# Shorter and fewer unread fp32 products in the long product stretches of TensorE

## Chip, cores and metric

The kernel runs on one core of one Trainium2 chip. Its time is device microseconds of that core, and a comparison is made between medians of several executions.

## The reference

Two networks are applied one after the other to x, 512 tokens of width 1024. Cut to what matters here:

```
def first_block(x, ...):
    for l in range(2):
        m = even_mixer(x, ...) if l % 2 == 0 else odd_mixer(x, ...)
        x = layer_norm(ALPHA * x + m, ...)
        x = layer_norm(ALPHA * x + conv_ffn(x, ...), ...)

def second_block(x, mem, ...):
    x = x + hybrid_mixer(rms_norm(x), ...)               # SSD scan, windowed attention, two gated branches
    x = x + memory_cross_attention(rms_norm(x), rms_norm(mem), w_q, w_kv, w_o)
    x = x + swiglu_ffn(rms_norm(x), w_in, w_out)
    return rms_norm(x, norm_final_g)
```

Nearly all of the arithmetic is in the products with large fp32 weight matrices: the two mixers' projections in and out, two convolutional feed-forward blocks (1024 to 5632 and 2816 back to 1024), the memory's keys and values, the hybrid mixer's input, its branches and its output, the cross attention's projections, and a last feed-forward block.

## The kernel before

**Units and tiles.** All weight matrices come as one stream of 405 units of 128 x 1024 fp32 (8 blocks of 128 x 128), 512 KB each, through a ring of four slots. SyncE issues the loads, ScalarE rounds a unit to `w_hi` (L323), VectorE forms the remainder `w_lo` (L329), and TensorE uses both. An output tile has 128 output channels and 512 tokens. For each block of 128 input channels `product_tile` issues three terms, `w_hi` with x high, `w_hi` with x low, `w_lo` with x high, each as two products of 256 columns (L357): six products a block, 48 a unit. In the profile they stand as groups of four with `w_hi` and two with `w_lo`.

**Stages.** TensorE walks the stages in a fixed order that is written out by hand (`pe_stages`): even_in, retention and stick-breaking attention, even_out, up0, down0, odd_in, differential attention, odd_out, up1, down1, norms with the memory's keys and values (xkv), bcdt, ssd, br_ssd, qkv, windowed attention, br_attn, mix_out, cross attention, xout, ffn_in, ffn_out. Products of layer-norm tails and heads are issued by `half_tile` (L388), those of two attention stages in parts (L1362), those of the memory from L1710.

**Plain fp32 products.** Small work (transposes, sums over partitions by a matrix of ones, attention scores) runs as plain fp32 products. In the profile one such product stands as two records, so a pair of them is four.

**The unread products.** `settle(pe, bank)` (L334 to L337) issues two fp32 products, ones by 256 columns of ones, into a bank of `ps` that nobody reads then. `product_tile` calls it when its argument `spare` names a bank, at the places of `SETTLE` (L332): ahead of block 0, term 0, and ahead of block 4, term 1. `spare` is given once in each of six stages, in an early tile: even_in (bank 3, tile (1, 1)), up0, odd_in and up1 (`head_pe`, bank 4, tile (1, 1)), br_ssd (bank 3, j == 1) and br_attn (bank 0, j == 1). That is 6 stages x 2 places x 2 products = 24 products. In down1, after tile 4, `mem_sum_pe` sums the memory over partitions (one fp32 product of 256 columns, L1653), and one unread product of 256 columns follows it (L1129). The stage xout has none; `xout_pe` issues its tiles 2 to 7.

Of the kernel before, what the change touches and what calls it, by code (L numbers as in the profile page):

```python
# [26 lines left out]
P = 128  # L27
# [31 lines left out]
UB, TB = {}, {}  # L59
# [22 lines left out]
CONST = {}  # L82
# [12 lines left out]
HALF = 256  # L95
# [93 lines left out]
def ffn_stage_numbers(stage):  # L189

    return {"up0": 0, "down0": 0, "up1": 1, "down1": 1, "ffn_in": 2, "ffn_out": 2}[stage]


def build(nc, dram, out):
    ctx = ExitStack()
    with ctx:
# [12 lines left out]
        const = ctx.enter_context(nc.sbuf_tensor("const", [P, N_CONST], F32))  # L209
        small = ctx.enter_context(nc.sbuf_tensor("small", [P, 128], F32))  # L210
        acc = [ctx.enter_context(nc.psum_tensor(f"acc{b}", [P, S], F32)) for b in range(2)]
        ps = ctx.enter_context(nc.psum_tensor("ps", [P, 6, S], F32))
        ident = const[:, CONST["ident"]:CONST["ident"] + P]
        ones = const[:, CONST["ones"]:CONST["ones"] + P]
# [68 lines left out]
        def ev(name):  # L283
            name = SHARED.get(name, (name, 0))[0]
            if name not in s:
                s[name] = sem(name)
            return s[name]
# [41 lines left out]
            dve.tensor_tensor(w_lo[:, u.slot], w_raw[:, u.slot], w_hi[:, u.slot].bitcast(F32),  # L329
                              ALU.subtract).then_inc(lo_done, 1)  # L330

        SETTLE = ((0, 0), (4, 1))  # L332

        def settle(pe, bank):  # L334

            for _ in range(2):
                pe.matmul(ps[:, bank, 0:HALF], ones, const[:, CONST["ones"]:CONST["ones"] + HALF], start=True, stop=True)  # L337

        def product_tile(pe, u, t, hi, lo, blocks=(8,), n=S, ready=None, spare=None):


            pe.wait_ge(acc_free[t.bank], t.in_bank + 1)
            a, k, total = acc[t.bank], 0, sum(blocks)
            parts = [slice(at, at + HALF) for at in range(0, n, HALF)]
            for m in blocks:
                pe.wait_ge(lo_done, u.count + 1)
                for b in range(m):
                    if ready is not None:
                        pe.wait_ge(ev(ready[0]), ready[1] + k + 1)
                    wh = w_hi[:, u.slot, b * P:(b + 1) * P]  # L350
                    wl = w_lo[:, u.slot, b * P:(b + 1) * P]
                    for term, (w, x) in enumerate(((wh, hi), (wh, lo), (wl, hi))):
                        if spare is not None and (k, term) in SETTLE:
                            settle(pe, spare)
                        for h in parts:

                            mm = pe.matmul(a[:, h], w, AR[:, x + k, h], start=(k == 0 and w is wh and x == hi and h.start == 0),  # L357
                                           stop=(k == total - 1 and w is wl), skip_group_check=True)
                    k += 1
                mm.then_inc(units_used, 1)  # L360
                u = u + 1
# [10 lines left out]
        def half_tile(pe, u, t, hi, lo, blocks, h, start=True, free=True, done=False, tail=False,  # L372
                      ready=None, between=()):


            if free:
                pe.wait_ge(acc_free[t.bank], t.in_bank + 1)
            a, k, total = acc[t.bank], 0, sum(blocks)
            cols = slice(HALF * h, HALF * h + HALF)
            for n, m in enumerate(blocks):  # L380
                pe.wait_ge(lo_done, u.count + 1)
                for b in range(m):
                    if ready is not None:
                        pe.wait_ge(ev(ready[0]), ready[1] + k + 1)
                    wh = w_hi[:, u.slot, b * P:(b + 1) * P]
                    wl = w_lo[:, u.slot, b * P:(b + 1) * P]
                    for w, x in ((wh, hi), (wh, lo), (wl, hi)):
                        mm = pe.matmul(a[:, cols], w, AR[:, x + k, cols], start=(start and k == 0 and w is wh and x == hi),  # L388
                                       stop=(k == total - 1 and w is wl), skip_group_check=True)
                    k += 1  # L390
                if done:
                    mm.then_inc(units_used, 1)
                elif tail and n == len(blocks) - 1:
                    mm.then_inc(ev("tail_a"), 1)
                if n < len(between):
                    between[n](pe)
                u = u + 1
# [7 lines left out]
        def tail_pe(pe, stage, hi, lo, blocks, c):  # L405
            r, per = TAIL[stage], len(blocks)
            norm = [lambda e: ln_sum_pe(e, c, 0, stage), lambda e: ln_var_pe(e, c, 0)]
            for h in range(2):
                for n in range(KD - r, KD):
                    between = norm[n - (KD - r):][:1] if per == 1 else norm  # L410
                    half_tile(pe, Units(UB[stage] + per * n), tail_tile(stage, n, h), hi, lo, blocks, h,
                              done=(h == 1), tail=True, between=between if h == 1 else ())
# [707 lines left out]
        def down_pe(pe, stage):  # L1120
            f = ffn_stage_numbers(stage)
            for j in range(KD - TAIL.get(stage, stage == "ffn_out")):
                product_tile(pe, Units(UB[stage] + 3 * j), Tiles(TB[stage] + j), GH, GL, DOWN,
                             ready=None if j else ("g_lo", KF * f))
                if stage == "down1" and j == 2:
                    mem_pe(pe)
                if stage == "down1" and j == 4:
                    mem_sum_pe(pe)
                    pe.matmul(ps[:, 1, 0:HALF], ones, const[:, CONST["ones"]:CONST["ones"] + HALF], start=True, stop=True)  # L1129
            if stage in TAIL:  # L1130
                tail_pe(pe, stage, GH, GL, DOWN, 1)
            if stage == "ffn_out":

                u = Units(UB[stage] + 3 * (KD - 1))
                half_tile(pe, u, Tiles(TB[stage] + KD - 1), GH, GL, DOWN, 0, tail=True)
                half_tile(pe, u, Tiles(TB[stage] + KD), GH, GL, DOWN, 1, done=True,
                          between=(lambda e: final_sum_pe(e, 0),))
                final_sum_pe(pe, 1)
# [4 lines left out]
        def final_sum_pe(pe, h):  # L1143
            pe.wait_ge(ev("sq_sum"), (KD - 1) * 4)
            pe.matmul(ps[:, 2 + h, 0:HALF], ones, A[:, SQ_SUM, last_half(h)], start=True, stop=False)
            pe.wait_ge(ev("rms_sq"), nth("rms_sq", KD * 4 + h))
            pe.matmul(ps[:, 2 + h, 0:HALF], ones, A[:, TMP + 4 + (KD - 1) % 2, last_half(h)], start=False,
                      stop=True).then_inc(ev("rms_sum"), 1)
# [494 lines left out]
        def mem_pe(pe):  # L1643
            pe.wait_ge(ev("mem_in"), 16)
            for k in range(KD):
                for c in range(MC):
                    mm = pe.transpose(mem_ps(k)[:, P * c:P * c + P],
                                      A[:, MEM_RAW + 2 * c + k // 4, (k % 4) * P:(k % 4 + 1) * P], ident)
                mm.then_inc(ev("mem_t"), 1)

        def mem_sum_pe(pe):
            pe.wait_ge(ev("mem_add"), nth("mem_add", KD))
            pe.matmul(ps[:, 2, 0:MEM], ones, A[:, MEM_SUM, 0:MEM], start=True, stop=True).then_inc(ev("mem_var"), 1)  # L1653
# [932 lines left out]
        XQ, XK, XV, XOH, XOL, X_SOFT, X_TURN = 16, 40, 48, 24, 32, TMP, 56  # L2586
# [199 lines left out]

        def xout_pe(pe):
            for n in range(2, KD):
                product_tile(pe, Units(UB["xout"] + n), Tiles(TB["xout"] + n), XOH, XOL)


        def ffn_pe(pe):
# [24 lines left out]
        def ffn_dve(dve):  # L2817
# [22 lines left out]
            input_pe, even_in_pe, ret_sb_pe,  # L2840
            lambda e: mixer_out_pe(e, "even_out", 8),
            lambda e: up_pe(e, "up0"), lambda e: down_pe(e, "down0"),
            odd_in_pe, diff_pe,
            lambda e: mixer_out_pe(e, "odd_out", 16),
            lambda e: up_pe(e, "up1"), lambda e: down_pe(e, "down1"),
            norms_pe, bcdt_pe, ssd_pe, br_ssd_pe,
            qkv_pe, win_pe, br_attn_pe, mix_pe, xattn_pe, xout_pe,
            ffn_pe, lambda e: down_pe(e, "ffn_out"),
        ]
        act_stages = [  # L2850
# [284 lines left out]
```

## Time and profile before

| | |
|---|---|
| median of 3 runs | 2666.0 us (2664.82 to 2670.92) |
| the profiled execution, its time | 2669.54 us |
| its span, first to last instruction | 2667.7 us |
| TensorE busy | 2593.1 us, 97% |
| VectorE, ScalarE busy | 1481.7 us, 1241.3 us |
| mean granted TensorE clock | 0.991 of full |
| bytes read from memory | 267 MB, 104 GB/s |
| unread products, L337 and L1129 | 48 and 2 records, 12.3 and 0.6 us of modelled busy time |

Busy time of TensorE overlaps from one product to the next, so the duration of one product (277 ns for 256 columns) is no price. The distance between the starts of successive products is: a group's time in the chain of work that ended last, divided by its count, or the distance between two starts in the timeline.

### The profile page before, as it was taken

How to read it: one execution, taken by the hardware profiler on the slowest of the kernel's cores; microseconds unless marked ns; L12 is line 12 of the kernel's file. 1: busy time of each engine (PE TensorE's matmuls, PEld its weight loads, DVE VectorE, ACT ScalarE, POOL GpSimd, SP SyncE). 2: the span in 40 equal slices, each digit the busy share in tenths (PEclk: the TensorE clock that was granted, in tenths of full speed). 3: DMA queues.
4: the chain of work that ended last, by engine and by line, in shares of the span. 5: the costliest groups of instructions: out<-in, count | busy, mean ns of one | idle time of the engine just before them, and what ended most of it. 6: DMA issues, size and time to landing. Idle time of an engine off the chain costs nothing.

```text
span 2667.7 us, 51033 instructions
## 1 busy us (share of the span) xinstructions
PE 2593.1 (97%) x20954; PEld 2395.1 (90%) x20954; DVE 1481.7 (56%) x2490; ACT 1241.3 (47%) x2037; POOL 118.0 (4%) x185
## 2 busy tenths in 40 slices
PE   8999999999999999999999999989999999999998
PEld 8985999999996699999989776779966998999998
DVE  5234666653426776664467989852476445544433
ACT  4336344432426644442365887842475243444422
POOL 0000000000000000000001233300000000000000
PEclk9999999999999999999999999999999999999999
DMA  7950233333331023333354566633311331333332
GB/s 195 116 84 1 64 104 96 98 105 107 111 96 48 25 74 102 95 97 118 105 195 142 183 197 193 198 109 96 93 50 56 96 127 48 96 96 100 95 103 72
DMA packets 75784, 279.02 MB, mean 105 GB/s; under 512 B 9402, under 2 KB 11610, under 8 KB 75088
## 3 DMA queue, kind: packets, MB, share of 16 engines
q1 hardware_dynamic: 62112, 217.42, 25.6%
q0 software_dynamic: 13488, 58.88, 10.0%
q8 instruction: 147, 2.41, 0.4%
q14 instruction: 37, 0.30, 0.0%
HBM read 267.03 MB, written 9.24 MB: 104 GB/s over the span
## 4 chain that ended last, share of the span: by engine, by line
PE 80%; DVE 11%; ACT 5%; issue 2%; DMA 1%; POOL 0%; DVEq 0%; ACTq 0%; SPq 0%
PE acc L357 66%; PE acc L388 3%; DVE big L1862 2%; DVE res_tmp L2161 1%; PE ps L388 1%; PE acc L1710 1%; DVE big L2492 1%; PE acc L1362 1%; DVE res_tmp L2155 1%; DVE w_lo L329 1%; PE ps L473 1%; DVE big L1514 1%; PE ps L779 1%; ACT res_tmp L2131 1%; ACT w_hi L323 1%
## 5 line engine op out<-in xcount | busy, mean ns | idle before, releaser
L357 PE MATMUL acc<-x_split,w_hi 128*128 128x256 f32 x7936 | 1234.0, 277 | 5.2 <-DVE big L1862 3.3
L357 PEld LDWEIGHTS acc<-x_split,w_hi 128*128 128x128 f32 x7936 | 1053.0, 188 | 8.2 <-issue 7.2
L357 PE MATMUL acc<-x_split,w_lo 128*128 128x256 f32 x3968 | 774.1, 276 | 0.0
L329 DVE TENSOR_TENSOR w_lo<-w_raw,w_hi 128x1024 fp32r<-128x1024 f32 x405 | 494.2, 1221 | 474.7 <-ACT w_hi L323 474.6
L323 ACT ACTIVATE w_hi<-w_raw 128x1024 fp32r<-128x1024 f32 x405 | 427.0, 1055 | 557.9 <-PE acc L357 519.9
L357 PEld LDWEIGHTS acc<-x_split,w_lo 128*128 128x128 f32 x3968 | 598.9, 188 | 0.0
L357 PE MATMUL acc<-big_r,w_hi 128*128 128x256 f32 x3376 | 523.4, 277 | 0.8 <-DVE big_r L2545 0.8
L357 PEld LDWEIGHTS acc<-big_r,w_hi 128*128 128x128 f32 x3376 | 447.7, 188 | 1.7 <-DVE big_r L2545 0.9
L357 PE MATMUL acc<-big_r,w_lo 128*128 128x256 f32 x1688 | 330.0, 277 | 0.0
L357 PEld LDWEIGHTS acc<-big_r,w_lo 128*128 128x128 f32 x1688 | 254.9, 188 | 0.0
L1076 ACT ACTIVATE res_tmp<-acc,par 128x512 f32<-128x512 f32 x84 | 64.9, 773 | 137.3 <-PE acc L357 132.9
L1101 DVE SCALAR_TENSOR_TENSOR res_tmp<-acc,par,res_tmp 128x511 f32<-128x511 f32 x84 | 62.8, 748 | 89.1 <-ACT res_tmp L1076 88.9
L2131 ACT ACTIVATE res_tmp<-res_tmp 128x256 f32<-128x256 f32 (+3 forms) x192 | 91.1, 550 | 34.2 <-DVE res_tmp L2155 34.0
L2161 DVE TENSOR_TENSOR res_tmp<-res_tmp 128x640 f32<-128x640 f32 x96 | 81.5, 885 | 14.0 <-ACT res_tmp L2131 13.6
L1862 DVE SCALAR_TENSOR_TENSOR big<-acc,par,big 128x510 f32<-128x510 f32 (+1 forms) x96 | 71.8, 748 | 11.5 <-ACT big L1852 8.8
L388 PE MATMUL acc<-big_r,w_hi 128*128 128x256 f32 x432 | 77.0, 282 | 0.5 <-DVE res_tmp L553 0.5
L1081 ACT ACTIVATE res_tmp<-res_tmp 128x512 f32<-128x512 f32 x44 | 27.8, 633 | 89.5 <-DVE small L1109 89.5
L1104 DVE SCALAR_TENSOR_TENSOR res_tmp<-acc,par,res_tmp 128x510 f32<-128x510 f32 x84 | 62.8, 748 | 11.7 <-DVE res_tmp L1101 0.3
L388 PEld LDWEIGHTS acc<-big_r,w_hi 128*128 128x128 f32 x432 | 66.3, 189 | 1.3 <-DVE res_tmp L553 0.9
L388 PE MATMUL acc<-big_r,w_lo 128*128 128x256 f32 x216 | 60.1, 278 | 0.0
L1978 POOL DMA_DIRECT2D res_tmp<-scratch_rows x96 | 51.3, 540 | 176.1 <-PE ps L2019 151.4
L1114 DVE TENSOR_TENSOR big_r<-res_tmp,big_r 128x512 f32 (+1 forms) x44 | 30.5, 693 | 43.8 <-ACT big_r L1083 43.8
(360 smaller groups left out, 2761.4 us busy)
## 6 DMA issues: line engine op xcount, KB each, us to landing
w_raw<-in_stream SPq DMA_DIRECT2D x405, 512.0 KB, 3.6
res_tmp<-scratch_rows POOLq DMA_DIRECT2D x96, 320.0 KB, 5.3
big<-scratch_rows POOLq DMA_DIRECT2D x32, 320.0 KB, 5.7
scratch_bias<-res_tmp POOLq DMA_DIRECT2D x8, 320.0 KB, 13.6
res_tmp<-in_x SPq DMA_DIRECT2D x2, 1024.0 KB, 6.9
res_tmp<-scratch_bias POOLq DMA_DIRECT2D x8, 256.0 KB, 4.0
scratch_x<-res_tmp POOLq DMA_DIRECT2D x1, 2048.0 KB, 8.9
scratch_kv<-big POOLq DMA_DIRECT2D x1, 2048.0 KB, 10.3
```

Of the source, the lines that this page charges most:

```text
L323: act.activation(w_hi[:, u.slot], w_raw[:, u.slot], ACT.Copy).then_inc(hi_done, 1)
L329: dve.tensor_tensor(w_lo[:, u.slot], w_raw[:, u.slot], w_hi[:, u.slot].bitcast(F32), ALU.subtract).then_inc(lo_done, 1)
L357: mm = pe.matmul(a[:, h], w, AR[:, x + k, h], start=(k == 0 and w is wh and x == hi and h.start == 0), stop=(k == total - 1 and w is wl), ...
L388: mm = pe.matmul(a[:, cols], w, AR[:, x + k, cols], start=(start and k == 0 and w is wh and x == hi), stop=(k == total - 1 and w is wl), s ...
L1076: act.activation(x, acc[t.bank][:], ACT.Identity, bias=col(f"cb{f}", tile), scale=col(f"cw{f}", tile + 88)).then_inc(ev("conv_now"), 1)
L1101: dve.scalar_tensor_tensor(x[:, 1:S], a[:, 0:S - 1], col(f"cw{f}", tile + 44), x[:, 1:S], ALU.mult, ALU.add).then_inc(ev("conv_tap1"), 1)
L1104: dve.scalar_tensor_tensor(x[:, 2:S], a[:, 0:S - 2], col(f"cw{f}", tile), x[:, 2:S], ALU.mult, ALU.add).then_inc(acc_free[t.bank], 1)
L1114: dve.tensor_tensor(AR.at(GL, 2 * i + q), prod, AR.at(GH, 2 * i + q).bitcast(F32), ALU.subtract).then_inc(ev("g_lo"), 1)
L1862: ins = dve.scalar_tensor_tensor(o, i, col("cw2", m + 24 * j), o, ALU.mult, ALU.add)
L1978: pool.dma_start(part(f, b, c), src).then_inc(ev(row_in(f, c)), 16)
L2131: ins = act.activation(w, w, ACT.Exp, bias=tab[:, 0, c, head:head + 1])
L2161: dve.tensor_tensor(w, w, cb, ALU.mult).then_inc(ev("s_w"), 1)
```

## The change

`SETTLE` keeps its first place alone, so each `spare` tile has one pair of unread products in place of two pairs. Each unread product has 128 columns in place of 256. In down1 a whole `settle` (two products of 128 columns) stands behind the memory's sum, where one product of 256 columns stood. Tile 2 of xout gets a pair (bank 0). No wait, no transfer and no other instruction is changed.

```diff
-        SETTLE = ((0, 0), (4, 1))
+        SETTLE = ((0, 0),)
 
         def settle(pe, bank):
 
             for _ in range(2):
-                pe.matmul(ps[:, bank, 0:HALF], ones, const[:, CONST["ones"]:CONST["ones"] + HALF], start=True, stop=True)
+                pe.matmul(ps[:, bank, 0:P], ones, const[:, CONST["ones"]:CONST["ones"] + P], start=True, stop=True)
...
                 if stage == "down1" and j == 4:
                     mem_sum_pe(pe)
-                    pe.matmul(ps[:, 1, 0:HALF], ones, const[:, CONST["ones"]:CONST["ones"] + HALF], start=True, stop=True)
+                    settle(pe, 1)
...
         def xout_pe(pe):
             for n in range(2, KD):
-                product_tile(pe, Units(UB["xout"] + n), Tiles(TB["xout"] + n), XOH, XOL)
+                product_tile(pe, Units(UB["xout"] + n), Tiles(TB["xout"] + n), XOH, XOL, spare=0 if n == 2 else None)
```

## Rows read from the trace of the kernel before

**Rows 1.** The page: engines, granted clock in 40 slices, shares of the chain.

```profile
PE 2593.1 (97%) x20954; PEld 2395.1 (90%) x20954; DVE 1481.7 (56%) x2490; ACT 1241.3 (47%) x2037; POOL 118.0 (4%) x185
...
PEclk9999999999999999999999999999999999999999
...
PE 80%; DVE 11%; ACT 5%; issue 2%; DMA 1%; POOL 0%; DVEq 0%; ACTq 0%; SPq 0%
```

**Rows 2.** Chain in order of time, long stretches: start us, us, what, count.

```profile
48.39 122.19 PE acc L357 x1078
...
350.91 313.95 PE acc L357 x2770
664.86 10.20 PE acc L388 x90
...
724.94 100.44 PE acc L357 x886
...
996.75 254.12 PE acc L357 x2242
...
1781.89 176.60 PE acc L357 x1558
...
2055.12 73.24 PE acc L357 x646
```

**Rows 3.** Timeline of TensorE, even_in: start us, modelled us, line, tiles, count.

```profile
42.18 0.62 PE L357 MATMUL acc<-x_split,w_hi 128*128 128x256 f32 x4
...
42.86 0.62 PE L357 MATMUL acc<-x_split,w_hi 128*128 128x256 f32 x4
...
43.54 1.02 PE L337 MATMUL ps<-const 128*128 128x256 f32 x4
...
45.10 0.62 PE L357 MATMUL acc<-x_split,w_hi 128*128 128x256 f32 x4
...
45.78 0.62 PE L357 MATMUL acc<-x_split,w_hi 128*128 128x256 f32 x4
...
46.46 0.62 PE L357 MATMUL acc<-x_split,w_hi 128*128 128x256 f32 x4
...
47.37 1.02 PE L337 MATMUL ps<-const 128*128 128x256 f32 x4
...
48.70 0.62 PE L357 MATMUL acc<-x_split,w_hi 128*128 128x256 f32 x4
```

**Rows 4.** Timeline of TensorE in ssd, round an fp32 pair of 128 columns.

```profile
1552.51 0.66 PE L2054 MATMUL ps<-const,big 128*128 128x128 f32 x4
...
1553.70 0.62 PE L357 MATMUL acc<-x_split,w_hi 128*128 128x256 f32 x4
...
1554.38 0.62 PE L357 MATMUL acc<-x_split,w_hi 128*128 128x256 f32 x4
```

**Rows 5.** Chain in order of time: behind eight and more fp32 records.

```profile
1250.86 1.75 PE ps L1647 x16
1252.61 31.09 PE acc L357 x264
...
1765.88 11.31 PE acc L357 x96
...
2255.64 3.43 PE ps L2653 x8
...
2263.31 39.58 PE acc L357 x336
```

**Rows 6.** Chain in order of time: behind four fp32 records.

```profile
301.26 2.74 PE acc L388 x24
...
317.80 2.83 PE acc L388 x24
...
1284.57 44.90 PE acc L357 x396
...
2304.61 338.66 PE acc L357 x2988
```

## The prediction

> **What bounds the kernel.** I read the page first. TensorE is busy 97% of the span and has 80% of the chain of work that ended last, and the clock digit is 9 in all forty slices, the full level of 2.4 GHz but for short stretches [rows 1]. So an instruction taken from TensorE in a dense stretch is time taken from the kernel, unless something else becomes late. Then I went through the chain in order of time, because there a group's time over its count is the true distance between starts. The reader is to see in it that the same product of 256 columns runs at two paces. In the long stretches 122.19 / 1078, 313.95 / 2770, 254.12 / 2242 and 176.60 / 1558 all give 113.3 to 113.4 ns [rows 2]. Elsewhere 31.09 / 264, 39.58 / 336 and 11.31 / 96 give 117.8 ns [rows 5]. The clock is full in both, no wait stands inside these groups, and a stretch keeps the pace with which it starts until TensorE is interrupted. The difference is 4.45 ns a product, 0.21 us a unit of 48.
>
> What chooses the pace is the thing to predict. Each of the six stages with unread products runs at the short pace behind them [rows 2], also br_ssd, which stood at 117.8 ns just ahead of them (1765.88 [rows 5]). Behind long runs of plain fp32 products the long pace is usual: 16 records of L1647, 8 of L2653 [rows 5]; of the 17 places where a run of eight or more equal records with full weights leads directly into products, 14 go on at the long pace. Behind four records the short pace is usual: x396 behind the pair in down1, which stood at 117.8 ns ahead of it [rows 5, 6], and x2988 at 113.3 ns [rows 6]. It isn't certain: of six pairs in the layer-norm heads four give 2.74 or 2.73 us for 24 products and two give 2.83, which is 117.9 ns each [rows 6]; both of these two come where TensorE had idled between products a moment before. A pair inside an unbroken stream has given the short pace at each of its 20 places, twelve of them the pairs of L337.
>
> **The second pair.** Between the first and second pairs of even_in the groups of six start at 45.10, 45.78 and 46.46: 0.68 us for six, 113.3 ns, so already the short pace [rows 3]. The other five stages show the same 0.68 there. In this trace the second pair gives nothing. Its price: without it the six-groups from 46.46 would follow at 0.68, so 48.70 would be 47.82. That is 0.88 us, and the first pair costs 45.10 - 42.86 - 1.36 = 0.88 us as well [rows 3]. Six second pairs are 6 x 0.88 = 5.3 us, all on TensorE, with nothing beside it that would hide them.
>
> **Half the columns.** The price of 0.88 us is four records and a restart of the stream. Plain fp32 records go by their columns: eight of 512 (L2653) take 3.43 us, 429 ns each, so 215 for 256 columns, and 16 of 128 (L1647) take 1.75 us, 109 ns each [rows 5]. Four records at 109 instead of 215 ns save 0.42 us, which leaves 0.46 us a pair. As the other bound, the nearest whole case is a pair of 128 columns in ssd: L2054 starts at 1552.51 and the six-group at 1553.70, where one six of 0.68 lies between, so 0.51 us [rows 4]; 0.05 of that belongs to the wider product ahead of it, so I take 0.46. Six first pairs save 6 x 0.42 = 2.5 us (2.2 with the upper bound).
>
> Does a pair of 128 columns choose the short pace too? The only cases are those in ssd. Sixteen such pairs stand directly ahead of products, and 15 of them go on at 0.68 us for six, as here from 1553.70 to 1554.38 [rows 4]; the one that does not (0.71 us) comes directly behind eight records of 512 columns, so it belongs with the long runs. Against it: there the stream had been broken by other fp32 work, while the new pairs stand inside a stream. Number of records, and not their time, is what separates the cases: the four records of 512 columns ahead of the x2988 (L1560 and L1562) take as long as eight of 256 would, and give the short pace [rows 6]. I take the short pace for all six stages.
>
> The Trainium skill ("TensorE: Matmul & The Clock Gate", Back-to-back issue gap) gives one spacing for a width, columns over 2.4 plus 2.5 ns, 109.2 ns for 256. The trace has 113.3 and 117.8 ns in its place, two values, so the rule misses what the change is about. By it pace would never be at stake, xout's pair would be a pure cost of 0.46 us, and the sum would be 5.3 + 2.5 - 0.5 = 7.3 us, 2658.7 us.
>
> **down1.** One unread product of 256 columns goes (two records, 430 ns) and two of 128 come (four records, 436 ns), with one restart as before. I take nothing; the bounds are a gain of 0.1 us, if a restart behind narrow records is shorter, and a loss of 0.1, if it is longer as in ssd. But with the memory's sum there are now six records in a row, between the four that give the short pace and the eight that give the long. If it falls to the long pace, 396 products [rows 6] cost 1.8 us. I keep this for the range.
>
> **xout.** The stretch from 2263.31 is seven tiles (336 products) at 117.8 ns [rows 5]; the pair comes ahead of the second of them, so 288 products go to 113.35 ns, a gain of 1.28 us, for 0.46 us. Net gain 0.8 us; a loss of 0.5 if the pair doesn't act.
>
> **What could hide or follow.** No wait is added, and no instruction stands behind a new one but the products themselves. The unread product writes a bank on TensorE alone. The suppliers keep up: a unit of 48 products takes 5.44 us, VectorE and ScalarE are busy 56% and 47% [rows 1], and the ring is four units deep, so 0.9 us once in a stretch finds no one late. The stages behind the stretches start from TensorE's last tile, so they move up with it.
>
> **Sum.** 5.3 + 2.5 + 0 + 0.8 = 8.6 us off. The profiled execution took 2669.54 us (span 2667.7 us), so it would be 2660.9 us. The median of the runs shown, 2666.0 us, is 3.5 us under the profiled one, and the forecast for the median is 2666.0 - 8.6 = 2657.4 us, 0.33% less. Places that restart behind an idle TensorE may choose their pace anew with shifted times; those with over 200 products are worth 1 to 2 us each, of both signs, so I put 3 us round the sum. For this kernel a change under 0.2% (5.3 us) can hardly be told from none.
>
> **Rivals.**
> The first is that the short pair leaves the pace as it finds it. For it: its four records take 0.44 us where the wide ones took 0.86, and the cases in ssd came behind broken streams. Then even_in, up0, odd_in and up1 stay short, as they were ahead of the first pair (42.18 to 42.86 is 0.68 us [rows 3]), but br_ssd (about 1584 products with the 26 between the pairs) and br_attn (672) stay long [rows 2, 5], and xout and down1 with them: (1584 + 672 + 288 + 396) x 4.45 ns = 13.1 us, and the time is 2670.5 us, the same within 0.2%. Beside it stands a rule of the Trainium skill (same page, What happens when you issue a matmul): the queue pulls weight loads ahead of products in flight, so an interruption would act by the time that it gives the queue; no row shows that queue.
>
> The second ends on the other side: the short pair puts the stream on the long pace, as the 16 records of 128 columns of L1647 did [rows 5]. The six stretches hold 1078 + 2770 + 90 + 886 + 2242 + 1558 + 646 = 9270 products [rows 2]. At 4.45 ns they cost 41.3 us, with xout and down1 44.3, and the time is 2701.7 us, 1.3% slower. It decides as soon as the loss passes 14 us, which up0 (12.7 us) does together with any other. Against it speak the 15 pairs in ssd.
>
> The third is that one stretch misses: the dropped second pair was its second throw. up0 alone gives 2670.1, up1 (10.0 us) 2667.4, br_ssd (7.0) 2664.4, even_in (4.8) 2662.2, odd_in (3.9) 2661.3, br_attn (3.0) 2660.4 us: mostly the same within 0.2%. Two of six head pairs missed [rows 6], but none of those within a stream.
>
> **Chances.** Forecast 0.70, pace left as found 0.08, long pace 0.07, one stretch missed 0.13, others 0.02. Faster by over 0.2% needs 2660.7 us or less: 0.64 of the 0.70 and 0.02 of the missed stretch, 0.66. Slower takes the 0.07, two missed stretches and the rest, 0.11. Same 0.23. The likeliest case alone spans 2654 to 2661 us. The range of 8 in 10 goes from 2653 to 2671 us: it takes in the first and third rivals and leaves out the second.
>
> **What the profile after would show.** L337 with 32 records of 128 columns, 109 ns apart (four in each of the six stages, in xout and in down1), none of 256 and no L1129. In the timeline about 0.46 us at each place. In the chain 113.3 ns a product behind each pair, in br_ssd and xout with 117.8 ahead of it. The prediction is wrong if a stretch of [rows 2] gives 117.8 ns, by 4.45 ns times its count, and its size is wrong if the restart behind narrow records is longer than in ssd.

## The result and the profile after

The changed kernel takes 2686.65 us in the median of 12 runs (2671.74 to 2698.26), the kernel before 2667.01 us (2664.16 to 2670.92, 12 runs). The ratio is 1.0066 with an interval of 1.005 to 1.0082: slower by two thirds of a per cent, where 0.33% faster was forecast, and outside the range of 2653 to 2671 us. (The two medians divide to 1.0074; the ratios in this text are those recorded with the runs.) The single times spread over 27 us, those of before over 7 us. That spread is itself a finding, and is taken up below. Three executions of the kernels below took thousands of us (one with two narrow pairs, two with one wide pair and xout); the medians of those kernels are taken without them.

The page of the changed kernel, in the lines that answer to [rows 1]:

```profile
PE 2612.1 (97%) x20936; PEld 2418.0 (90%) x20936; DVE 1482.6 (55%) x2490; ACT 1241.0 (46%) x2037; POOL 118.3 (4%) x185
...
PEclk9999999999999999999999999999999999999999
```

The clock digit is 9 throughout (mean 0.993 of full), the other engines do the same work, and TensorE is busy 19 us longer although it has fewer columns to pass. The chain of work in order of time says where (start us, us, what, count), and answers to [rows 2] and [rows 5]:

```profile
44.19 130.03 PE acc L357 x1104
...
344.36 5.66 PE acc L357 x48
350.46 316.90 PE acc L357 x2796
717.22 5.44 PE acc L357 x48
723.10 107.43 PE acc L357 x912
...
989.54 5.44 PE acc L357 x48
995.43 267.13 PE acc L357 x2268
...
1296.27 44.90 PE acc L357 x396
...
1776.49 10.90 PE acc L357 x96
1787.39 0.44 PE ps L337 x4
1787.83 186.58 PE acc L357 x1584
...
2060.84 5.65 PE acc L357 x48
2066.49 0.45 PE ps L337 x4
2066.93 79.17 PE acc L357 x672
...
2281.06 0.44 PE ps L337 x4
2281.50 38.10 PE acc L357 x336
```

Each time over its count is the distance between starts. Five of the six stretches of [rows 2] now run at 117.8 ns: 130.03 / 1104, 107.43 / 912, 267.13 / 2268, 186.58 / 1584, 79.17 / 672. Only up0 keeps 113.3 ns (316.90 / 2796). The reader is to look at the tile ahead of each pair too. up0 was long there (5.66 / 48 = 117.9) and is short behind the pair; odd_in (5.44 / 48 = 113.3), up1 and br_ssd (10.90 / 96 = 113.5) were short and are long behind it. xout went from long to short. The timeline further down shows even_in short ahead of its pair. So the narrow pair turned the pace over at six of its seven places. The seventh is br_attn: long ahead (5.65 / 48 = 117.7) and long behind. What sets it apart comes out with the table below.

How that adds up, as the differences of starts in the two chains: at even_in's end the changed kernel is 3.6 us late (44.19 + 130.03 against 48.39 + 122.19), at up0's end 2.5, at odd_in's end 5.2, ahead of up1's pair 2.9, at its end 11.7, at br_ssd's pair 10.2, at its end 15.9, at br_attn's end 17.7, and behind xout 16.7 us, which is the difference of the profiled times (2686.26 - 2669.54). A long stretch costs its count times 4.45 ns less the 1.3 us that the pairs save: up1 10.1 - 1.3 = 8.8, measured 11.7 - 2.9 = 8.8.

The timeline of TensorE round the pair of even_in, answering to [rows 3]:

```profile
42.90 0.62 PE L357 MATMUL acc<-x_split,w_hi 128*128 128x256 f32 x4
...
43.58 0.60 PE L337 MATMUL ps<-const 128*128 128x128 f32 x4
...
44.74 0.63 PE L357 MATMUL acc<-x_split,w_hi 128*128 128x256 f32 x4
...
45.44 0.63 PE L357 MATMUL acc<-x_split,w_hi 128*128 128x256 f32 x4
```

From 42.90 to 43.58 six products take 0.68 us, from 44.74 to 45.44 they take 0.70 to 0.71. The pair costs 44.74 - 43.58 - 0.71 = 0.45 us, as estimated. So the price of a pair was right and the pace was wrong.

### The profile page after: what moved, and what is told of

The parts are those of the page before. It is cut to its first block, busy times and chain, and to the rows that moved or that the text cites. A ratio compares the mean times of both kernels' runs of the same rounds, so it can differ in the third digit from the quotient of the medians.

```text
span 2684.5 us, 50997 instructions
## 1 busy us (share of the span) xinstructions
PE 2612.1 (97%) x20936; PEld 2418.0 (90%) x20936; DVE 1482.6 (55%) x2490; ACT 1241.0 (46%) x2037; POOL 118.3 (4%) x185
## 4 chain that ended last, share of the span: by engine, by line
PE 82%; DVE 10%; ACT 4%; issue 2%; DMA 1%; POOL 0%; DVEq 0%; SPq 0%; ACTq 0%
PE acc L357 67%; PE acc L388 3%; DVE big L1862 2%; PE ps L388 1%; DVE res_tmp L2161 1%; PE acc L1710 1%; DVE big L2492 1%; DMA res_tmp<-scratch_rows 1%; PE acc L1362 1%; DVE big L1514 1%; DVE w_lo L329 1%; PE ps L473 1%; PE ps L779 1%; DVE res_tmp L2155 1%; PE ps L767 1%
## 5 line engine op out<-in xcount | busy, mean ns | idle before, releaser
L357 PE MATMUL acc<-x_split,w_hi 128*128 128x256 f32 x7936 | 1248.5, 280 | 4.5 <-DVE big L1862 2.6
L357 PEld LDWEIGHTS acc<-x_split,w_hi 128*128 128x128 f32 x7936 | 1068.5, 189 | 6.8 <-issue 6.5
L357 PE MATMUL acc<-x_split,w_lo 128*128 128x256 f32 x3968 | 782.8, 279 | 0.0
L1862 DVE SCALAR_TENSOR_TENSOR big<-acc,par,big 128x510 f32<-128x510 f32 (+1 forms) x96 | 71.8, 748 | 10.1 <-ACT big L1852 7.5
L1104 DVE SCALAR_TENSOR_TENSOR res_tmp<-acc,par,res_tmp 128x510 f32<-128x510 f32 x84 | 62.9, 749 | 11.7 <-DVE res_tmp L1101 0.3
```

Source lines behind the costliest of these rows:

```text
L1104: dve.scalar_tensor_tensor(x[:, 2:S], a[:, 0:S - 2], col(f"cw{f}", tile), x[:, 2:S], ALU.mult, ALU.add).then_inc(acc_free[t.bank], 1)
L1862: ins = dve.scalar_tensor_tensor(o, i, col("cw2", m + 24 * j), o, ALU.mult, ALU.add)
```

## The experiments

All kernels but the first three have one place in each of the six stages and one in xout (seven places), and down1 as before unless said. "Short" is 113.3 ns a product, "long" 117.8. Times beside which nothing stands are medians, and each profile is of one execution; the kernel before was timed beside each group, at 2667.51, 2667.17 and 2667.57 us.

**One wide pair.** `SETTLE = ((0, 0),)` alone, 256 columns.

```diff
-        SETTLE = ((0, 0), (4, 1))
+        SETTLE = ((0, 0),)
```

> The second pairs are left out, the first ones keep 256 columns; down1 and xout are as before. Theory W (width): a pair of 256 columns gives the short pace (113.3 ns a product) from either pace ahead, a pair of 128 columns does not, so here all six stretches are short and the time is 6 x 0.88 = 5.3 us below before, about 2661.7 us, 0.2% faster. Theory S (second throw): the loss of the changed kernel comes from the dropped second pair, so one or more of the six stretches runs at 117.8 ns here too and the time is 5 to 20 us above before.

Measured: 2662.36 us, ratio 0.9982 (0.9972 to 0.9992). All six stretches are short, for example br_ssd:

```profile
1771.46 179.55 PE acc L357 x1584
```

5.2 us are saved where 6 x 0.88 = 5.3 were worked out. The second pair did nothing, and theory S (second throw) falls. even_in stood long ahead of its pair here (117.8 ns, last distance 121 ns), so the one wide pair did turn a long stretch.

**Two narrow pairs.** Both places stay, with 128 columns.

```diff
             for _ in range(2):
-                pe.matmul(ps[:, bank, 0:HALF], ones, const[:, CONST["ones"]:CONST["ones"] + HALF], start=True, stop=True)
+                pe.matmul(ps[:, bank, 0:P], ones, const[:, CONST["ones"]:CONST["ones"] + P], start=True, stop=True)
```

> Both places of SETTLE stay, with 128 columns in place of 256; down1 and xout are as before (down1's unread product keeps 256). Theory W (width, a random throw each time): five of eight narrow pairs missed in the changed kernel, so the stretches are a mixture here and the time is 5 to 30 us above before. Theory T (toggle): in the changed kernel a narrow pair gave the other pace in seven of eight cases (short to long four times, long to short three), so a second one, 26 products later, turns the long pace back to the short one; the four head stretches (even_in, up0, odd_in, up1) end short, and the time is about 5 us below before where it is short ahead of the first pair. Theory S: two throws are enough, 5 us below before.

Measured: 2673.39 us, ratio 1.0015 (1.0002 to 1.0028). The chain in order of time, first odd_in, then br_ssd:

```profile
717.78 5.66 PE acc L357 x48
723.88 2.97 PE acc L357 x26
727.29 104.37 PE acc L357 x886
...
1779.00 10.89 PE acc L357 x96
1789.89 0.44 PE ps L337 x4
1790.34 3.07 PE acc L357 x26
1793.41 0.44 PE ps L337 x4
1793.85 176.63 PE acc L357 x1558
```

odd_in stands long ahead (5.66 / 48 = 117.9), is short between the pairs (2.97 / 26 = 114.2, the restart in it) and long behind the second (117.8). br_ssd is short, long between (3.07 / 26 = 118.1), and short. Eleven of the twelve pairs turned the pace over; the one that did not stands in br_attn, long ahead and long behind. Theory T (toggle) holds at these eleven and fails at the twelfth. Its time failed, since it took the heads to start short: in this execution even_in, odd_in and up1 start long and so end long.

**No pair.** `SETTLE = ()`.

> SETTLE is empty: no unread product in any of the six stages; down1 as before, xout none. Theory W and T: a stretch keeps the pace with which it starts, so those that were short ahead of their first pair in the trace of before (even_in, up0, odd_in, up1) stay short and br_ssd and br_attn stay long at a cost of 7.0 and 3.0 us, against 12 x 0.88 = 10.6 us saved: 0 to 1 us below before if the heads start short, up to 30 us above if they start long in this run. A rival: products without pairs drift to the long pace, all six stretches at 117.8 ns, 41 - 10.6 = 31 us above before.

Measured: 2671.15 us, with single times from 2654.87 to 2692.87, ratio 1.0019 (0.9994 to 1.0044), unclear. The chain:

```profile
38.16 130.78 PE acc L357 x1152
...
338.70 334.80 PE acc L357 x2844
...
992.89 262.76 PE acc L357 x2316
```

130.78 / 1152 and 262.76 / 2316 are 113.5 ns, 334.80 / 2844 is 117.7. br_ssd and br_attn are long as well. Nothing drifts, so the rival in the expectation falls. But up0 did not start long, as theories W and T would have it. Its first two tiles run at 113.3 ns, and in the timeline the change stands at a pause ahead of the third:

```profile
349.19 0.39 PE L357 MATMUL acc<-x_split,w_lo 128*128 128x256 f32 x2
...
349.58 0.74 PE L357 MATMUL acc<-x_split,w_hi 128*128 128x256 f32 x4
```

Two successive distances between starts are 274 and 221 ns there. The weight load at 349.58 stands behind 0.19 us of idle time that VectorE ended (L1104, which reads `acc`), so the tile waited for its bank. Behind the pause every distance is of the long pace. up1 has the same pause at 1003.49 (261 and 223 ns) and comes out of it short. So a pause alone can change the pace too, as this one case shows. In the thirteen other profiles, which have unread products in the tile before, the heads have no such pause.

The starts also differ between executions. Up to the first pair of even_in all kernels have the same code, and ahead of it even_in is short in six of the fourteen profiles and long in eight. No kernel was profiled twice, so that the spread of the single times comes from such draws is argued from this and not seen. What the wide pairs are worth here: the best time without them is 8 us under the lowest of before beside it (2662.61), the worst 22 us over its highest (2670.64).

**One wide pair, xout too.** The changed kernel with 256 columns put back, down1 as before.

```diff
         SETTLE = ((0, 0),)
...
-                product_tile(pe, Units(UB["xout"] + n), Tiles(TB["xout"] + n), XOH, XOL)
+                product_tile(pe, Units(UB["xout"] + n), Tiles(TB["xout"] + n), XOH, XOL, spare=0 if n == 2 else None)
```

> One pair of 256 columns in each of the six stages and one ahead of tile 2 of xout; down1 as before. Theory W: all seven stretches short behind their pair, 5.3 us saved and 0.4 us more from xout (288 products x 4.45 ns less 0.88 us) if xout starts long, so 5 to 6 us below before, 2660 to 2662 us. Theory S: as in the run with one wide pair, 5 to 20 us above before.

Measured: 2660.14 us, ratio 0.9978 (0.9968 to 0.9988). All seven short:

```profile
2253.41 0.86 PE ps L337 x4
2254.28 38.10 PE acc L357 x336
```

This kernel differs from the changed one in the width of the pairs and in down1 (which was short in both) and is 26.5 us faster in the median. So the narrowing of both products is the cause of the loss.

**One product of 256.** From here the pair of the last kernel is varied and nothing else.

```diff
-            for _ in range(2):
+            for _ in range(1):
```

> One product of 256 columns in place of the pair at the seven places (six stages and xout), the rest as in the run with one wide pair and xout. Theory R (restart: the width of the last plain record ahead of the stream decides): the last record has 256 columns, so all seven stretches are short, each place costs 0.45 us in place of 0.88, and the time is 7 x 0.43 = 3.0 us below that run, about 2658 us. Theory D (duration: the stream must be held up for some 0.86 us of plain records): 0.43 us is as short as the narrow pair, so the pace is turned over instead, stretches that start short end at 117.8 ns, and the time is 10 to 35 us above.

Measured: 2710.66 us, ratio 1.0161 (1.0144 to 1.0178). Six of seven stretches are long, also two that were long ahead, for example xout:

```profile
2292.47 0.43 PE ps L337 x2
2292.91 39.58 PE acc L357 x336
...
2334.20 351.92 PE acc L357 x2988
```

The width of the last record does not decide (theory R falls), and the pace is not turned over as under theory D either. The last row is ffn_in and ffn_out behind the four records of L1560 and L1562: 117.8 ns, in this profile alone, which is 13.3 us of its time. The table below comes back to it.

**Four products of 128.**

```diff
-            for _ in range(2):
-                pe.matmul(ps[:, bank, 0:HALF], ones, const[:, CONST["ones"]:CONST["ones"] + HALF], start=True, stop=True)
+            for _ in range(4):
+                pe.matmul(ps[:, bank, 0:P], ones, const[:, CONST["ones"]:CONST["ones"] + P], start=True, stop=True)
```

> Four products of 128 columns (eight records) in place of the pair of 256 at the seven places, the same columns and about the same time on TensorE. Theory D (duration): all seven stretches short, the time equals that of the run with one wide pair and xout, 2661 us. Theory R (width of the last record): as with two products of 128, a short stream goes on long and a long one short, 10 to 35 us above. Theory N (number of records, my prediction's): eight records give the long pace from either side, up to 44 us above.

Measured: 2694.74 us, ratio 1.0102 (1.0081 to 1.0123). The chain at even_in, up0 and xout:

```profile
42.77 0.89 PE ps L337 x8
43.66 125.14 PE acc L357 x1104
...
339.45 5.44 PE acc L357 x48
344.89 0.89 PE ps L337 x8
345.78 329.31 PE acc L357 x2796
...
2290.82 0.89 PE ps L337 x8
2291.71 38.10 PE acc L357 x336
```

The wide pair takes 0.86 us and these four 0.89, and they turn the pace over as two narrow ones do (even_in and xout stood long ahead, up0 short; br_attn stayed long here too). So it isn't the time for which the stream is held up (theory D falls), nor that eight records lead to the long pace from either side (theory N falls: even_in and xout went to short).

**Narrow, then wide; wide, then narrow.** The same four records in both orders.

```diff
-            for _ in range(2):
-                pe.matmul(ps[:, bank, 0:HALF], ones, const[:, CONST["ones"]:CONST["ones"] + HALF], start=True, stop=True)
+            for cols in (P, HALF):
+                pe.matmul(ps[:, bank, 0:cols], ones, const[:, CONST["ones"]:CONST["ones"] + cols], start=True, stop=True)
```

(the second kernel has `(HALF, P)`)

> The pair's first product has 128 columns, its second 256, at the seven places. Theory R: the last record is wide, so all seven are short, at 0.88 - 0.21 = 0.67 us a place, 1.5 us below the run with one wide pair and xout, about 2659.5 us. Theory D: between the narrow and the wide pair, undecided. Theory N (four records): short.

> The pair's first product has 256 columns, its second 128, at the seven places; the same records as in the run before this one in the other order. Theory R: the last record is narrow, so the pace is turned over as by two narrow products, with stretches at 117.8 ns and 10 to 35 us above the run with one wide pair and xout. Theory D: the same result as with the narrow product first. Theory N: short, 2659.5 us.

Measured: 2698.61 us, ratio 1.0109 (1.0084 to 1.0133), with narrow first; 2660.01 us, ratio 0.9973 (0.9963 to 0.9984), with wide first. The chain at up0, narrow first:

```profile
349.82 0.65 PE ps L337 x4
350.48 329.32 PE acc L357 x2796
```

and wide first:

```profile
344.04 0.65 PE ps L337 x4
344.69 316.89 PE acc L357 x2796
```

Both take 0.65 us, and 2796 products behind them take 12.4 us more in the one than in the other. Only the order differs. Theories R and D are both contradicted by this pair of kernels. With the wide product first all seven are short, of which four stood long ahead.

**Wide then narrow, in down1 too.** The unread product behind the memory's sum has 128 columns.

```diff
-                    pe.matmul(ps[:, 1, 0:HALF], ones, const[:, CONST["ones"]:CONST["ones"] + HALF], start=True, stop=True)
+                    pe.matmul(ps[:, 1, 0:P], ones, const[:, CONST["ones"]:CONST["ones"] + P], start=True, stop=True)
```

> The pair of 256 and then 128 columns at the seven places, and in down1 the unread product behind the memory's sum of 256 columns has 128 too, which makes the same order there. Theory P (a wide product first and exactly one more behind it gives the short pace from either side): all eight places short, 0.2 us below the run with wide then narrow, 2660 us or a little less, 0.25% below before. If down1 misses, 396 products cost 1.8 us.

Measured: 2660.75 us, ratio 0.9973 (0.9963 to 0.9984). All eight short. 0.2 us can't be told from none here, and the ratio is that of the kernel above.

**Wide, then 64 columns.** `for cols in (HALF, P // 2)`.

> The pair is 256 and then 64 columns at the seven places, down1 as before. Theory P: all seven short, and 0 to 0.1 us a place cheaper than with 128, 2659 to 2660 us. Theory Q (the second product has to have at least 128 columns, or it acts like none, as the single product of 256 did): long in most stretches, 30 to 45 us above before.

Measured: 2695.05 us, ratio 1.0093 (1.0075 to 1.0111), 27.5 us above before, a little under the 30 to 45 of theory Q. The five stretches that stood short went long, br_attn stayed long, xout went from long to short. Theory P falls as it was put (a wide product and any one behind it). Theory Q's count of columns stands, but the second product did not act like none: it made six of the seven stretches turn over as the narrow pair does.

**Three and four wide products.** `range(3)` and `range(4)` with 256 columns.

> Three products of 256 columns (six records) at the seven places. Theory L (length of the run of plain records): three lie between two, which give the short pace, and four and eight, which mostly gave the long one in the stages of the kernel before; if only one product is too few, three are short and the time is 7 x 0.43 = 3.0 us above the run with one wide pair and xout, 2664 us. Theory P: more than one product behind the first one spoils it, long, 30 to 45 us above before.

> Four products of 256 columns (eight records) at the seven places. Theory L and theory P: the long pace in all or most stretches, as behind L473 (16 records) and L2636 (8 records) in the kernel before, 45 us above before. A rival: those runs gave the long pace for what they read and wrote and not for their length, so four unread products are short, 7 x 0.86 = 6.0 us above the run with one wide pair and xout, 2667 us.

Measured: three 2698.26 us, ratio 1.0117 (1.0102 to 1.0133); four 2708.45 us, ratio 1.0154 (1.0138 to 1.017). The chain at up0 and br_ssd with three:

```profile
345.74 1.29 PE ps L337 x6
347.03 329.32 PE acc L357 x2796
...
1789.94 11.31 PE acc L357 x96
1801.26 1.29 PE ps L337 x6
1802.55 179.55 PE acc L357 x1584
```

up0 went long; br_ssd went from long (11.31 / 96 = 117.8) to short. With four, all seven are long, from either side. Theory L falls at three, and holds at four: unread products do there what the eight records of L2636 did, so what those read and wrote isn't needed for it.

All of it together, each place of L337 in each profile counted by the pace ahead and behind. The starts in the traces show that the distances of the long pace repeat in a cycle of three: in even_in of the changed kernel every third is 118.3 ns in the mean and the two between are 117.5. A pair can fall at three points of the cycle. The last distance ahead of it is 116 or 117 ns at one, 120 or 121 at the second, and 121 or 122 at the third, where the slowest distance of the cycle stands just before it. The column "121 ns" holds the second point, and in the row 128 + 128 the third as well, four cases each. No other unread sequence met the third point.

| pair at the place | short ahead | long, 121 ns | long, 117 ns |
|---|---|---|---|
| 256 + 256 (before and two kernels) | short 21 of 21 | short 3 of 3 | short 1 of 1 |
| 256 + 128 (two kernels) | short 6 of 6 | short 4 of 4 | short 4 of 4 |
| 128 + 128 (changed, two narrow pairs) | long 9 of 9 | short 8 of 8 | long 2 of 2 |
| 128 x 4 | long 4 of 4 | short 2 of 2 | long 1 of 1 |
| 128 + 256 | long 5 of 5 | short 1 of 1 | long 1 of 1 |
| 256 + 64 | long 5 of 5 | short 1 of 1 | long 1 of 1 |
| 256 x 3 | long 3 of 3 | short 3 of 3 | long 1 of 1 |
| 256 x 1 | long 4 of 4 | long 2 of 2 | short 1 of 1 |
| 256 x 4 | long 4 of 4 | long 2 of 2 | long 1 of 1 |

Each cell has one outcome only, though several hold one or two cases. As far as they go, at a place inside a stream the pace behind follows from the sequence and from where in its cycle the stream is cut, and only two of the nine sequences give the short pace at each point that they met.

That is not from everywhere. Other plain products in these fourteen traces do meet the third point, once for each of two wide sequences, and both times the stream goes on long. One is the pair of 256 + 256 columns of a layer-norm sum (L465 and L467), in the kernel with 256 + 64, between these two rows of 10.60 / 90 = 117.8 and 2.83 / 24 = 117.9 ns:

```profile
681.95 10.60 PE acc L388 x90
...
693.41 2.83 PE acc L388 x24
```

The other is the pair of 512 columns (L1560 and L1562) ahead of the 2988 products in the kernel with one product of 256. At the other two points and out of the short pace, pairs of 256 or 512 columns inside a stream gave the short pace at every place in the fourteen traces. So a wide pair can miss at the third point, by one case each, and for 256 + 128 that point is untried.

Why the two sequences give the short pace where they do is not settled: width of the first or the last, time, and number of records are each contradicted by a row. The kernel with the wide and then the narrow product beats both kernels of the case, the one before by 0.27%. Against one wide pair and xout it is not shown to be faster (ratios 0.9973 and 0.9978, intervals overlapping).

## Why the prediction was wrong

**The step that failed** is "Number of records, and not their time, is what separates the cases", and with it "I take the short pace for all six stages". Five of the six ran at 117.8 ns instead, 29.1 us by count. The changed kernel shows four records of 128 columns turning short into long; the kernels with (128, 256) and (256, 128), both four records, go opposite ways. The 15 of 16 pairs of L2054 in ssd [rows 4] were no evidence, as the argument against it had said: they stand behind other plain products, not inside a stream. Nor are they pairs. The kernel issues four transposes there, and the trace has 64 records for 64 transposes. A transpose stands as one record, not as two like the other plain fp32 products, and so it is for the 16 of L1647. L2054's four records start 109 ns apart, those of L337's narrow pair 108, 110 and 112 ns. In the changed kernel these transposes mostly still lead to the short pace, while L337's pairs of the same width do not. I had the right objection and gave it too small a chance.

**The pace ahead** was taken as a matter for one rival alone. In the trace of before ten of the twelve pairs of L337 stood in a stream that was short already, so they showed that a wide pair keeps the short pace, and only two that it makes it (one at each of two points of the cycle). That a pair could spoil a short stream had only the rival of the long pace (0.07), which put all six stretches at 2701.7 us. The truth lies between it and the rival of the pace left as found: a swap, whose result depends on how the stretch starts. The starts differ between executions, as even_in shows, and the spread of 27 us fits that. I had named the swap nowhere.

**The second pair** gave nothing, as said: 5.2 us saved for 5.3 worked out, in the kernel with one wide pair.

**The narrow pair's price** was 0.45 us for 0.46 worked out.

**down1** is short behind six records in a row, as it was behind four. It stood long ahead; that the same six records keep a stream short was not tried.

**xout** went from long to short, but its term was mis-sized: I counted the first of the seven tiles of [rows 5] as standing ahead of the pair, and all 336 products stand behind it. The seventh is the first tile of ffn_in, ahead of L1560. The gain is 336 x 4.45 ns - 0.45 = 1.0 us for 0.8. That is luck: the narrow pair turned xout the right way because the profiled execution stood long there, at a point of the cycle where it turns.

**The sum.** Expected saving by its own terms 5.3 + 2.5 + 1.0 = 8.8 us; five long stretches (6540 products x 4.45 ns) cost 29.1 us; that makes 20.3 us over the profiled execution of before, and 16.7 were measured. The rest, some 3.6 us, lies in stages between the stretches: 2.2 us between odd_in's end and up1's pair and 1.5 us between up1's end and br_ssd's pair, by the starts above. Of the 2.2 us, 1.0 is 216 products ahead of up1 that ran short in place of long (16.33 for 16.97 us and 8.45 for 8.76), and 1.4 lies in the differential attention ahead of them. The cause of that part, and of the 1.5 us, is open.

**The rule of the Trainium skill** ("TensorE: Matmul & The Clock Gate", Back-to-back issue gap) would have made the pace no question. By it the time would be 2658.7 us. The page gives that formula for a product by itself; for streams in which each product has its weight load it gives about 81 ns at 128 columns and 131 ns at 512, again one value for a width. The runs show two distances, 113.3 and 117.8 ns, for one width at the full clock.

## What to carry to other kernels

A long stream of equal products can run at two steady paces and keep one for hundreds of microseconds, until something interrupts it, so read time over count in the chain for every stretch, not the busy share or the duration of one product. A cheap trick that puts the stream on its good pace is to be tested from both paces ahead of it, at every point of their cycle, and in every part of its form: here (256, 128) worked at all 14 places, (128, 256) spoiled each of the five streams that were short. Evidence for such a trick from other instructions counts only if they are the same instructions in the same surroundings. A kernel whose single times spread much wider than before may have something that is drawn anew at each execution; one profile of it is one draw.

## What the runs showed of the hardware

TensorE's step for products of 256 columns with new weights each, at the full granted clock of 2.4 GHz, is 113.3 or 117.8 ns, and in the profiled stretches of 300 to 3000 products it did not change while nothing else was issued and TensorE did not pause. At a pause, with two distances of 274 and 221 ns, it changed once (up0 of the kernel without pairs).

Two unread products, four records, choose between the two, and the order of the same records decides: 316.89 us for 2796 products behind (256, 128), 329.32 us behind (128, 256).

Plain fp32 records of 128 columns start 108 to 112 ns apart, of 256 columns 215 ns, and of 64 columns less again: the (256, 64) pair takes 0.60 us in the chain, the (256, 128) pair 0.65. A plain fp32 product is two records, an fp32 transpose one.
